# Two-layer block in fp32r: operand halves sent through TensorE together, with the opening, the SSD/GLA order and the last gain rearranged

## The chip, the cores and the metric

The kernel runs on one core of one Trainium2 chip. The metric is device time in microseconds (us) of the whole program. Every matmul of a projection is done in the type float32r: a float32 operand is split into a high part (the value as float32r rounds it) and a low part (what is left), and three products (high by high, high by low, low by high) are accumulated in PSUM.

## What is computed

The program is two transformer-like blocks over 256 tokens (272 with 16 meta tokens in the first block) of width 1024, and a final norm. What the change touches is in these lines of the reference:

```python
# first block
h = xn @ w_in                                    # k, v, q, c, h, b, gates
out = merged @ w_out
u, g = jnp.split(xn @ w_up_gate, 2, axis=-1)     # 2 x 2816 columns
ffn = (jax.nn.gelu(causal_dwconv(u, w)) * g) @ w_down
# second block, layer one: SSD scan and gated linear attention (GLA)
u = h @ w_in                                     # z, x, B, C, dt, q, k, v, gates
out = jnp.concatenate([y_a, o_b], axis=-1) @ w_out
x = x + out
# second block, layer two: attention with a gate, then the final norm
x = x + (attention * gate) @ w_out
```

## The kernel before

**Operands.** Activations lie transposed in SBUF: 128 channels on the partitions, tokens along the free axis. `xhi`/`xlo` hold the high and low part of the normalised input of a stage (8 pieces `kt` of 128 channels), `yhi`/`ylo` those of the branch outputs; `fhi`/`flo` (22 pieces, FFN) and `ehi`/`elo` (16 pieces, second block) are views of the same buffers.

**Weights.** All weights come as one stream of 253 chunks of 128 x 1024 float32 (8 blocks of 128 x 128), in the order of `STREAM` (line 124). SyncE (SP) loads a chunk into one of 4 raw buffers. ScalarE (ACT) makes the high part (`split_hi`, L559), VectorE (DVE) the low part (`split_lo`, L1063), each into a ring of 4 (`RING`). `feed(tile)` on either engine splits as many chunks as the tile has, always the next in the stream, about four tiles ahead. A raw buffer is free when the low part is made, a ring slot when TensorE (PE) has read the chunk.

**Tiles.** A tile is 128 output channels. `project` (L1724) runs over its blocks and issues three matmuls a block, each with a 128 x 128 weight block as the stationary operand and 256 to 272 tokens as the moving one (L1749). For `ev` and `mv` the tokens are stationary and 256 or 512 weight columns move (L1752). `project_together` (L1759, L1777) takes three tiles at once where the input is still being made. Outputs rotate through PSUM banks 0 to 3; `bank_free` lets PE wait until the tile that used the bank before was read (`taken`). Tile names: `k v q c h b gc ga pc pa wo` (mixer), `fu fg fd` (up, gate, down projection of the FFN), `es eb ec ex eq ek ev ez eg eo1 eo2` (SSD and GLA layer, eo1 and eo2 being the two halves of its output projection), `mk mv mq mz mo` (last layer).

**Order.** Each engine has its own program written out by hand; semaphores join them. The places that matter:

- Opening: SP loads half of chunk 0, x in three pieces, the other half, chunk 1. ACT waits for the parameters (L591), makes the high parts (L600, L597), DVE the low parts (L1092, L1078). PE runs tile `k0`, then `k1`, `k2`, then the sum of squares `total(1, 0)` (L1788), then `k3`.
- FFN loop on DVE (L1338 to L1345), for tile pair `i`: `ffn_up` (L1313), `feed(fg i-1)`, `ffn_conv` (two operations, L1320), `ffn_out(i-1)` (L1328), `feed(fu i)`. GpSimd (POOL) scales the gelu (L443) and makes the low part of the result (L449).
- `out_tiles` (L1251): DVE copies each tile of `wo` and `fd` out of PSUM (L1259).
- SSD/GLA loop, `p` = 0 to 3 (DVE L1509, ACT L918, PE L2053): per `p` two SSD head pairs (`turn_x`, `ssd_heads`) and one GLA pair (`turn_keys`, `gla_scores`, `gla_kv`, `gla_out`, `gla_sums`) between the projections. POOL forms the arguments of the GLA exponentials (`gla_args`, L506, L508) and the products with queries and keys (L494, L496).
- Output projection of that layer on DVE: for `eo1` a multiply out of PSUM (L1594), a feed, an addition to H (L1602); for `eo2` `residual` (L1576): addition to H out of PSUM (L1580), feed, low part of the next input (`x_low_of`, L1078). ACT makes the high part and the square, POOL adds the squares (L435). The next tile `mk0` needs all eight pieces of that input.
- The tail: DVE adds `mo` to H (L1699), ACT squares and multiplies with the final gain (L1030, L1039), two sums (L2176, L2179), scaling (L1710), stores.

`d.settle()` makes DVE wait for its own last signalled operation.

Of the kernel before, what the change touches and what calls it, by code (L numbers as in the profile page):

```python
# [138 lines left out]
for _name, _n in (("g_pre_mix", 8), ("g_post_mix", 8), ("g_pre_ffn", 8), ("g_post_ffn", 8), ("even_norm", 8),  # L139
# [19 lines left out]
def build(nc, xT, params, weights, masks, gate_w2, out, scratch):  # L159
    with ExitStack() as ctx:  # L160
# [13 lines left out]
        xhi_t = sb("x_hi", KT * T, F32R)  # L174
        xlo_t = sb("x_lo", KT * T, F32R)
        YW = 3 * KT * NA
        yhi_t = sb("y_hi", YW, F32R)
        ylo_t = sb("y_lo", YW, F32R)
        h_t = sb("hidden", KT * T)
# [5 lines left out]
        rcol = sb("rinv_by_token", 4)  # L185
        arena = sb("arena", ARENA)
# [8 lines left out]
        xhi, xlo, H = v3(xhi_t[:], KT), v3(xlo_t[:], KT), v3(h_t[:], KT)  # L195

        yhi = yhi_t[:].rearrange("p (s a b) -> p s a b", s=3, a=KT)
        ylo = ylo_t[:].rearrange("p (s a b) -> p s a b", s=3, a=KT)
        fhi, flo = v3(yhi_t[:, 0:FT * L], FT), v3(ylo_t[:, 0:FT * L], FT)
        ehi, elo = v3(yhi_t[:, 0:16 * L], 16), v3(ylo_t[:, 0:16 * L], 16)  # L200
# [56 lines left out]
        fy = A4(2, L)  # L257

# [127 lines left out]
        HALF = {t: n for n, t in enumerate((s_, i_) for s_, i_, b_, n_ in STREAM if s_ in ("eb", "ec", "ex", "ez", "eg"))}  # L386
        CONVS = [t for t in HALF if t[0] in ("eb", "ec", "ex")]
        K_TAKEN = [taken[FIRST_OUT["ek", p]][1] for p in range(4)]
# [5 lines left out]
        def _(sp_):  # L394
            half = CW // 2
            cuts = (0, 2 * T, 4 * T, KT * T)

            def load_x(n):
                sp_.dma_start(h_t[:, cuts[n]:cuts[n + 1]], xT[:, cuts[n]:cuts[n + 1]]).then_inc(S(f"load_x{n}"), 16)

            sp_.dma_start(raw[:, 0:half], weights[0, :, 0:half]).then_inc(S("load_half"), 16)
            load_x(0)
            load_x(1)
            sp_.dma_start(raw[:, half:CW], weights[0, :, half:CW]).then_inc(S("raw0"), 16)
            load_x(2)
            for c in range(1, NCHUNKS):
# [17 lines left out]
        def _(pool):  # L424
# [87 lines left out]
            for p in range(4):  # L512
                if p:
                    ssd_weights(2 * p)
                else:
                    gla_args(0)
# [8 lines left out]
                if p:  # L525
                    ssd_add(2 * p)
# [1741 lines left out]
```

## Time and profile before

| | us |
|---|---|
| median of 3 runs | 850.49 (849.14 to 850.52) |
| the profiled execution, own time | 848.99 |
| its span | 847.2 |
| PE busy | 830.6 |
| DVE busy | 620.8 |
| ACT busy | 499.1 |
| POOL busy | 132.7 |

The span is what the trace shows from the first to the last instruction; 1.8 us of the execution lie outside it. A matmul's duration in the trace is its passage through the array and overlaps the next one; what it costs is the distance from its start to the start of the next. So cadences are read from starts, not from durations.

### The profile page before, as it was taken

How to read it: one execution, taken by the hardware profiler on the slowest of the kernel's cores; microseconds unless marked ns; L12 is line 12 of the kernel's file. 1: busy time of each engine (PE TensorE's matmuls, PEld its weight loads, DVE VectorE, ACT ScalarE, POOL GpSimd, SP SyncE). 2: the span in 40 equal slices, each digit the busy share in tenths (PEclk: the TensorE clock that was granted, in tenths of full speed). 3: DMA queues.
4: the chain of work that ended last, by engine and by line, in shares of the span. 5: the costliest groups of instructions: out<-in, count | busy, mean ns of one | idle time of the engine just before them, and what ended most of it. 6: DMA issues, size and time to landing. Idle time of an engine off the chain costs nothing.

```text
span 847.2 us, 16833 instructions
## 1 busy us (share of the span) xinstructions
PE 830.6 (98%) x6770; PEld 800.5 (94%) x6770; DVE 620.8 (73%) x1044; ACT 499.1 (59%) x842; POOL 132.7 (16%) x131
## 2 busy tenths in 40 slices
PE   8999999999999999999999999889999999999997
PEld 7999999999999999999999999779999999888896
DVE  6547888886666688667664488997887697568764
ACT  7346657555454576555554469668768555346655
POOL 1000000000000305433441100332534011000002
PEclk9999999999999999999999999999999999999999
DMA  8754434346555536656566535455454375554431
GB/s 326 233 153 139 152 106 173 127 137 179 183 188 186 173 106 191 201 177 186 189 197 196 180 100 171 142 170 167 150 167 157 112 231 183 186 169 141 126 101 50
DMA packets 39565, 139.81 MB, mean 165 GB/s; under 512 B 4400, under 2 KB 5056, under 8 KB 39360
## 3 DMA queue, kind: packets, MB, share of 16 engines
q1 hardware_dynamic: 37728, 135.78, 50.1%
q10 hardware_dynamic: 1760, 2.96, 1.1%
q8 instruction: 54, 0.88, 0.4%
q14 instruction: 23, 0.19, 0.1%
HBM read 137.65 MB, written 1.06 MB: 164 GB/s over the span
## 4 chain that ended last, share of the span: by engine, by line
PE 90%; DVE 5%; ACT 2%; DMA 1%; issue 1%; SPq 0%; DVEq 0%; ACTq 0%
PE ps L1749 71%; PE ps L1777 5%; PE ps L1752 5%; DVE weights_lo L1063 1%; PE ps L1870 1%; PE ps L1855 1%; PE ps L1884 1%; PE ps L2127 1%; PE ps L2145 1%; PE ps L1998 1%; DMA hidden<-xT_in 1%; PE ps L2135 1%; DVE arena L1375 1%; PE ps L2041 0%; PE ps L2050 0%
## 5 line engine op out<-in xcount | busy, mean ns | idle before, releaser
L1749 PE MATMUL ps<-x_hi,weights_hi 128*128 128x256 f32 (+3 forms) x1288 | 373.0, 290 | 5.4 <-DVE weights_lo L1063 3.0
L1063 DVE TENSOR_TENSOR weights_lo<-raw_weights,weights_hi 128x1024 fp32r<-128x1024 f32 x251 | 311.5, 1245 | 85.4 <-ACT weights_hi L559 85.3
L1749 PE MATMUL ps<-x_lo,weights_hi 128*128 128x256 f32 (+3 forms) x1288 | 363.8, 282 | 0.0
L1749 PE MATMUL ps<-x_hi,weights_lo 128*128 128x256 f32 (+3 forms) x1288 | 363.2, 282 | 0.0
L559 ACT ACTIVATE weights_hi<-raw_weights 128x1024 fp32r<-128x1024 f32 x251 | 263.8, 1053 | 152.8 <-PE ps L1749 62.2
L1749 PEld LDWEIGHTS ps<-x_hi,weights_hi 128*128 128x128 f32 x1288 | 242.9, 189 | 13.6 <-issue 10.9
L1749 PEld LDWEIGHTS ps<-x_lo,weights_hi 128*128 128x128 f32 x1288 | 242.9, 189 | 1.0 <-issue 0.7
L1749 PEld LDWEIGHTS ps<-x_hi,weights_lo 128*128 128x128 f32 x1288 | 243.4, 189 | 0.0
L1749 PE MATMUL ps<-y_hi,weights_hi 128*128 128x256 f32 (+1 forms) x488 | 137.7, 282 | 0.0
L1749 PE MATMUL ps<-y_lo,weights_hi 128*128 128x256 f32 (+1 forms) x488 | 137.4, 282 | 0.0
L1749 PE MATMUL ps<-y_hi,weights_lo 128*128 128x256 f32 (+1 forms) x488 | 137.1, 281 | 0.0
L435 POOL TENSOR_TENSOR arena<-arena 128x256 f32<-128x256 f32 (+1 forms) x24 | 25.9, 1078 | 494.8 <-ACT arena L708 328.2
L1749 PEld LDWEIGHTS ps<-y_hi,weights_hi 128*128 128x128 f32 x488 | 92.0, 189 | 0.3 <-issue 0.2
L1749 PEld LDWEIGHTS ps<-y_lo,weights_hi 128*128 128x128 f32 x488 | 91.9, 188 | 0.3 <-issue 0.2
L1749 PEld LDWEIGHTS ps<-y_hi,weights_lo 128*128 128x128 f32 x488 | 92.0, 189 | 0.0
L443 POOL TENSOR_TENSOR arena<-arena,rinv 128x256 f32<-128x256 f32 x22 | 32.9, 1496 | 81.6 <-ACT arena L751 81.4
L1752 PE MATMUL ps<-weights_hi,x_hi 128*128 128x256 f32 (+1 forms) x96 | 31.0, 323 | 0.0
L1752 PE MATMUL ps<-weights_lo,x_hi 128*128 128x256 f32 (+1 forms) x96 | 30.6, 319 | 0.0
L1752 PE MATMUL ps<-weights_hi,x_lo 128*128 128x256 f32 (+1 forms) x96 | 30.6, 318 | 0.0
L746 ACT ACTIVATE arena<-arena,params 128x256 f32<-128x256 f32 x22 | 11.1, 510 | 30.2 <-DVE arena L1313 30.2
L1313 DVE TENSOR_TENSOR arena<-ps,rinv 128x258 f32<-128x258 f32 x22 | 9.4, 428 | 25.1 <-PE ps L1749 24.5
L1320 DVE SCALAR_TENSOR_TENSOR arena<-arena,params 128x256 f32<-128x256 f32 x44 | 21.9, 498 | 4.2 <-ACT arena L746 1.0
(265 smaller groups left out, 1049.6 us busy)
## 6 DMA issues: line engine op xcount, KB each, us to landing
raw_weights<-weights_in SPq DMA_DIRECT2D x252, 512.0 KB, 3.7
arena<-decay_rows ACTq DMA_DIRECT2D x8, 256.0 KB, 3.6
masks<-masks_in SPq DMA_DIRECT2D x1, 1186.0 KB, 8.3
hidden<-xT_in SPq DMA_DIRECT2D x2, 272.0 KB, 4.1
hidden<-xT_in SPq DMA_DIRECT2D x1, 544.0 KB, 5.6
raw_weights<-weights_in SPq DMA_DIRECT2D x2, 256.0 KB, 4.0
gate_w<-gate_w_in ACTq DMA_DIRECT2D x1, 256.0 KB, 5.7
out<-arena ACTq DMA_DIRECT2D x1, 256.0 KB, 2.1
```

The lines of the kernel that those rows point to most:

```text
L435: ins = nc.gpsimd.tensor_tensor(sq[:, 0, t0:T], sq[:, 0, t0:T], sq[:, i, t0:T], ALU.add)
L443: g.sig(nc.gpsimd.tensor_tensor(fgl[:, i % 2, :], fgl[:, i % 2, :], rinv[:, META:T], ALU.mult), "gelu_scaled")
L559: a.sig(A(whi[:, s * CW:(s + 1) * CW], raw[:, (c % RAW) * CW:(c % RAW + 1) * CW], ACT.Copy), "hi_ready")
L746: a.sig(A(fcv[:, i % 2, :], fu[:, i % 2, 0:L], ACT.Copy, scale=pcol("conv_ffn", i)), "tap_ready")
L1063: d.sig(TT(wlo[:, s * CW:(s + 1) * CW], raw[:, (c % RAW) * CW:(c % RAW + 1) * CW], whi[:, s * CW:(s + 1) * CW].bitcast(F32), ALU.subtract) ...
L1313: d.sig(TT(fu[:, i % 2, :], r, rinv[:, TA:T], ALU.mult), "u_ready")
L1320: ins = STT(out=c_, in0=u[:, j:L + j], scalar=pcol("conv_ffn", FT * j + i), in1=c_, op0=ALU.mult, op1=ALU.add)
L1375: ins = STT(out=dst, in0=scr2[:, n % 2, j:L + j], scalar=pcol("even_conv", 10 * j + ct), in1=dst, op0=ALU.mult, op1=ALU.add)
L1749: ins = mm(bank(BANK_OF[no])[:, 0:b - a], wt, x_[:, kt, a:b], start=s0, stop=s1)
L1752: ins = mm(bank(BANK_OF[no + o])[0:t1 - t0, 0:step * P], x_[:, kt, t0:t1], wt, start=s0, stop=s1)
L1777: ins = mm(bank(BANK_OF[no])[:, 0:b - a], w_[:, at:at + P], x_[:, kt, a:b], start=kt == 0 and n == 0 and len(passes) == 2, stop=kt == KT - ...
L1855: ins = mm(bank(4 + e)[:, c0:c0 + T - t0], keysT[rows, p, k0:k0 + P], qpair[rows, p % 2, t0:T], start=n == 0, stop=n == 2, skip_group_chec ...
```

## The change

1. **Wide tiles.** `x_hi`/`x_lo` and `y_hi`/`y_lo` become the two halves of one buffer each. For the tiles in `WIDE` (fg 2 to 21, fd 0 to 6, eo1 3 to 6, eo2 0 to 6, mo 3 to 6) `project` issues two matmuls a block in place of three: the high weights against high and low tokens as one moving operand of 512 columns into a whole bank, then the low weights against the high tokens, 256 columns, added to the bank's first half. DVE joins the two halves of the bank when it reads the tile: one or two operations more a tile.
2. **Opening.** x comes in four pieces, the first two on ACT's DMA queue with the gain of the first norm in front of them; chunks 0 and 1 come in halves. PE takes `k0` and `k1` together, two pieces of x at a time (`first_keys`), and the sum of squares inside `k3`.
3. **FFN start.** `feed(fu1)` and `feed(fg1)` move one step forward on ACT and DVE.
4. **SSD/GLA loop, p = 0 and 1.** POOL's `gla_args` are gone; DVE makes small columns of biases (`decay_cols`) and ACT forms the exponentials in four pieces of 64 columns each. The products of p = 0 move from POOL to DVE (`first_products`). Gate work of p = 0 moves into p = 1 (`gate_both`). On PE `gla_scores(0)` follows `eq1`, `gla_kv(0)` follows `ek1`, `gla_out(0)` follows `ev1`, and `gla_sums(0)` follows `ez2`.
5. **Tail.** The last piece's multiplication with the final gain moves from ACT to DVE.

```diff
+        WIDE = ([("fd", i) for i in range(KT - 1)] + [("eo1", i) for i in range(3, KT - 1)]
+                + [("eo2", i) for i in range(KT - 1)] + [("mo", i) for i in range(3, KT - 1)]
+                + [("fg", i) for i in range(2, FT)])
...
+                        if tile in WIDE:
+                            b_ = bank(BANK_OF[no])
+                            mm(b_.rearrange("p (c t) -> p c t", c=2), whi[:, at:at + P], x_[:, :, kt, a:b], start=first,
+                               stop=last, skip_group_check=True)
+                            ins = mm(b_[:, 0:L], wlo[:, at:at + P], hi[:, kt, a:b], start=False, stop=last,
+                                     skip_group_check=True)
...
+            def low_part(tile):
+                return bank(BANK_OF[FIRST_OUT[tile]])[:, L:2 * L]
...
                     r = result((stage, i), 0, T - t0)
...
-                    d.sig(V.tensor_copy(mout[:, i, t0:T], r), "mout_ready")
+                    if (stage, i) in WIDE:
+                        d.step(V.tensor_copy(mout[:, i, t0:T], r))
+                        d.settle()
+                        d.sig(TT(mout[:, i, t0:T], mout[:, i, t0:T], low_part((stage, i)), ALU.add), "mout_ready")
+                    else:
+                        d.sig(V.tensor_copy(mout[:, i, t0:T], r), "mout_ready")
...
                 need(dve, "ffn_split", i - 1)
+                if ("fg", i) in WIDE:
+                    d.settle()
+                    d.step(V.tensor_copy(fsum, low_part(("fg", i))))
+                    d.settle()
+                    d.step(TT(fsum, r, fsum, ALU.add))
+                    d.settle()
+                    r = fsum
                 d.sig(TT(fy[:, i % 2, :], r, fgl[:, i % 2, :], ALU.mult), "ffn_y")
...
                     r = result((stage, i), 0, L)
                     d.settle()
+                    if (stage, i) in WIDE:
+                        d.step(TT(H[:, i, META:T], r, H[:, i, META:T], ALU.add))
+                        r = low_part((stage, i))
+                        d.settle()
                     d.sig(TT(H[:, i, META:T], r, H[:, i, META:T], ALU.add), "h_ready")
...
-                d.sig(TT(t_, r, rpost[:, 0:L], ALU.mult), "eo1_taken")
+                if ("eo1", i) in WIDE:
+                    d.step(V.tensor_copy(t_, r))
+                    d.settle()
+                    d.sig(TT(t_, t_, low_part(("eo1", i)), ALU.add), "eo1_taken")
+                    d.settle()
+                    d.step(TT(t_, t_, rpost[:, 0:L], ALU.mult))
+                else:
+                    d.sig(TT(t_, r, rpost[:, 0:L], ALU.mult), "eo1_taken")
...
+            def first_keys():
+
+                for n in range(4):
+                    for c in range(2):
+                        no = FIRST_OUT["k", c]
+                        if n == 0:
+                            pe.wait_ge(S("lo_half"), c + 1)
+                        if n == 2:
+                            pe.wait_ge(S("lo_ready"), c + 1)
+                        for kt in (2 * n, 2 * n + 1):
+                            pe.wait_ge(S("x_split"), kt + 1)
...
+            first_keys()
+            project(("k", 2), x2, 0, T)
+            project(("k", 3), x2, 0, T, first_total)
...
+            def first_products():
+                dve.wait_ge(S("gla_exp"), 1)
+                d.sig(TT(kb[:, 0, :], kb[:, 0, :], e_k[:, 0, :], ALU.mult), "gla_kl")
+                d.sig(TT(ka[:, 0, :], ka[:, 0, :], e_k[:, 0, :], ALU.mult), "gla_ka")
+                for e in range(2):
+                    rows = slice(64 * e, 64 * e + 64)
+                    d.step(TT(qg[rows, 0, e, :], eg[rows, 0, :], e_q[rows, 0, :], ALU.mult))
+                    ins = TT(qe[rows, 0, e, :], em[rows], e_q[rows, 0, :], ALU.mult)
+                    d.sig(ins, "gla_qk") if e else d.step(ins)
...
-                a.step(A(em, ka[:, k, :], ACT.Exp, scale=-1.0 / 16))
-                a.step(A(kb[:, k, :], kb[:, k, :], ACT.Exp, scale=-1.0 / 16))
-                a.settle()
-                a.step(A(ka[:, k, :], ka[:, k, :], ACT.Exp, scale=1.0 / 16))
+                for n, (dst, scale) in enumerate(((kb[:, k, :], 1.0 / 16), (ka[:, k, :], 1.0 / 16), (em, -1.0 / 16))):
+                    for c in range(4):
+                        w_ = slice(64 * c, 64 * c + 64)
+                        a.step(A(dst[:, w_], gcs[:, p, w_], ACT.Exp, scale=scale, bias=decay_cols[:, n, p, c:c + 1]))
...
+                if p == 1:
+                    project(("eq", 1), x2, META, T)
+                    gla_scores(0)
+                    project(("ek", 1), x2, META, T)
+                    turn_x(2)
+                    gla_kv(0)
+                    project(("ev", 1), x2, META, T, toks=toksL)
+                    ssd_heads(2)
+                    gla_out(0)
...
-                a.sig(A(fin[:, c, KT - 1, :], H[:, KT - 1, w_], ACT.Copy, scale=pcol("final_norm", KT - 1)), "gained")
...
+            d.step(TS(fin[:, :, KT - 1, :], H[:, KT - 1, META:T].rearrange("p (c t) -> p c t", c=2),
+                      pcol("final_norm", KT - 1), None, ALU.mult))
```

## Rows read from the trace of the kernel before

**Rows 1.** The page: busy time by engine, and the chain that ended last, by engine.

```profile
PE 830.6 (98%) x6770; PEld 800.5 (94%) x6770; DVE 620.8 (73%) x1044; ACT 499.1 (59%) x842; POOL 132.7 (16%) x131
PE 90%; DVE 5%; ACT 2%; DMA 1%; issue 1%; SPq 0%; DVEq 0%; ACTq 0%
```

**Rows 2.** Waits of PE: line, releaser, us in total, times, longest.

```profile
PE ps L1749 <- DVE weights_lo L1063: 3.0, 2, 2.4
PE ps L2041 <- DVE arena L1472: 2.4, 1, 2.4
```

**Rows 3.** Timeline of PE: start us, duration us, instruction; tile fd4 and mv.

```profile
460.98 0.27 PE L1749 MATMUL ps<-y_hi,weights_hi 128*128 128x256 f32 x1
...
468.75 0.28 PE L1749 MATMUL ps<-y_hi,weights_hi 128*128 128x256 f32 x1
...
730.23 0.40 PE L1752 MATMUL ps<-weights_hi,x_hi 128*128 128x512 f32 x1
...
750.14 0.39 PE L1752 MATMUL ps<-weights_lo,x_hi 128*128 128x512 f32 x1
```

**Rows 4.** Windows: length, busy us of PE, PEld, DVE, ACT, POOL, PE clock, DMA.

```profile
520.00:540.00 20.00, 19.48 (x160) 18.47 (x158) 18.44 (x32) 16.42 (x32) 1.13 (x2) 1.00 0.62 194
540.00:560.00 20.00, 16.59 (x124) 14.91 (x124) 18.97 (x28) 11.58 (x24) 8.56 (x9) 0.91 0.42 139
680.00:700.00 20.00, 20.00 (x172) 20.00 (x171) 18.93 (x27) 11.24 (x18) 3.21 (x4) 1.00 0.72 234
```

**Rows 5.** Timeline of the opening: DVE low parts, first matmul of k4.

```profile
5.30 0.69 DVE L1092 TENSOR_TENSOR weights_lo<-raw_weights,weights_hi 128x512 fp32r<-128x512 f32 x1 [5.30 <-ACT weights_hi L600]
5.91 1.73 DVE L1078 SCALAR_TENSOR_TENSOR x_lo<-hidden,params,x_hi 128x272 fp32r<-128x272 f32 x4
...
21.34 0.29 PE L1749 MATMUL ps<-x_hi,weights_hi 128*128 128x272 f32 x1
```

**Rows 6.** Timeline of the SSD/GLA loop, p = 0 and 1: PE, ACT, DVE.

```profile
542.08 0.36 PE L1749 MATMUL ps<-x_hi,weights_hi 128*128 128x256 f32 x1 [2.41 <-DVE weights_lo L1063]
...
540.41 0.42 ACT L892 ACTIVATE arena<-arena 128x256 f32<-128x256 f32 x1 [2.18 <-POOL arena L508]
...
537.47 1.27 DVE L1400 TENSOR_TENSOR_SCAN arena<-masks,arena 128x256 f32<-128x256 f32 x2
...
540.72 1.21 DVE L1063 TENSOR_TENSOR weights_lo<-raw_weights,weights_hi 128x1024 fp32r<-128x1024 f32 x1
...
573.81 0.36 PE L1749 MATMUL ps<-x_hi,weights_hi 128*128 128x256 f32 x1
```

**Rows 7.** Timeline of one FFN round on DVE, and a POOL scaling.

```profile
387.34 0.43 DVE L1313 TENSOR_TENSOR arena<-ps,rinv 128x258 f32<-128x258 f32 x1 [1.56 <-PE ps L1749]
...
390.26 1.22 DVE L1063 TENSOR_TENSOR weights_lo<-raw_weights,weights_hi 128x1024 fp32r<-128x1024 f32 x1
393.04 0.43 DVE L1313 TENSOR_TENSOR arena<-ps,rinv 128x258 f32<-128x258 f32 x1 [1.56 <-PE ps L1749]
...
390.54 1.53 POOL L443 TENSOR_TENSOR arena<-arena,rinv 128x256 f32<-128x256 f32 x1 [3.29 <-ACT arena L751]
```

**Rows 8.** Groups of DVE instructions by form: count, busy us, mean ns.

```profile
L1259 DVE COPY arena<-ps 128x256 f32<-128x256 f32 x8 | 3.4, 425 | 11.1 <-PE ps L1749 10.1 <-ACT arena L714 1.0
```

**Rows 9.** Timeline of eo1, eo2 and mk: DVE, then the first matmul of mk1.

```profile
678.65 0.43 DVE L1602 TENSOR_TENSOR hidden<-hidden,arena 128x256 f32<-128x256 f32 x1
679.18 0.42 DVE L1594 TENSOR_TENSOR arena<-ps,rinv_post 128x256 f32<-128x256 f32 x1
...
692.27 0.42 DVE L1580 TENSOR_TENSOR hidden<-ps,hidden 128x256 f32<-128x256 f32 x1
...
694.81 0.42 DVE L1580 TENSOR_TENSOR hidden<-ps,hidden 128x256 f32<-128x256 f32 x1
...
706.10 0.48 DVE L1078 SCALAR_TENSOR_TENSOR x_lo<-hidden,params,x_hi 128x256 fp32r<-128x256 f32 x1 [0.58 <-ACT x_hi L567]
...
707.85 0.47 PE L1749 MATMUL ps<-x_hi,weights_hi 128*128 128x256 f32 x1
```

More of the change, by code:

```diff
@@ L760, in _ @@
             ffn_gelu(0)
+            feed(("fg", 1))
             ffn_gelu(1)
[L762 removed]
             ffn_high(0)
@@ new lines, in gate_both @@
+            def gate_both(u):
+                z_full(("ez", u), zs[:, u % 2, :])
+                z_full(("eg", u), gs[:, u % 4, :])
+                gate_y(u)
+            dve.wait_ge(S("tkc_ready"), 1)
+            ssd_args(0)
+            ssd_weights(0)
+            split_lo()
+            z_full(("ex", 1), xs[:, 1, :], name="xsilu")
+            z_half(("ez", 0), zs[:, 0, :])
+            feed(("ez", 0))
+            ssd_y(0)
+            gate_sum()
+            decay_sums(0)
+            feed(("eg", 0))
@@ new lines, in _ @@
+            z_half(("eg", 0), gs[:, 0, :])
+            ssd_weights(1)
+            ssd_args(1)
+            conv_in(("ex", 2))
+            feed(("ex", 2))
+            first_products()
+            z_half(("ez", 1), zs[:, 1, :])
+            feed(("ez", 1))
+            conv_rest(("ex", 2), 2, xs[:, 2, :])
+            ssd_y(1)
+            z_half(("eg", 1), gs[:, 1, :])
+            gla_scores(0)
+            z_full(("ex", 2), xs[:, 2, :], name="xsilu")
+            feed(("eg", 1))
+            conv_in(("ex", 3))
@@ new lines, in _ @@
+            ssd_args(2)
+            gla_states(0)
+            feed(("ex", 3))
+            for p in range(1, 4):
+                u = 2 * p
+                take_queries(p)
+                if p == 1:
+                    take_keys(1)
+                    gate_both(0)
+                    feed(("eq", 1))
+                    conv_rest(("ex", 3), 3, xs[:, 3, :])
+                    ssd_y(2)
+                    feed(("ek", 1))
+                    z_full(("ex", 3), xs[:, 3, :], name="xsilu")
+                    gate_both(1)
+                    feed(("ev", 1))
+                    z_half(("ez", 2), zs[:, 0, :])
+                    ssd_args(3)
+                    gla_norm(0)
+                    feed(("ez", 2))
+                    ssd_low(0)
+                    ssd_low(1)
+                else:
@@ L2097, in last_scan @@
                     gla_out(3)
-            project_together([("eo1", i) for i in range(3)], ehi, elo, [(0, L)] * 3,
+            project_together([("eo1", i) for i in range(3)], e2, [(0, L)] * 3,
                              lambda kt: pe.wait_ge(S("ye_hi"), kt + 1),
@@ L2167, in _ @@
             together = 3
-            project_together([("mo", i) for i in range(together)], ehi, elo, [(0, L)] * together,
+            project_together([("mo", i) for i in range(together)], e2, [(0, L)] * together,
                              lambda kt: pe.wait_ge(S("mo_hi"), kt + 1),
```

443 lines of the change are left out of this document (228 added, 215 removed).

## The prediction

> **What bounds the kernel now.** I read the page first: PE is busy for 98% of the span and makes up 90% of the chain that ended last [rows 1]. So a microsecond counts only where PE issues fewer or cheaper passes, or waits less. The waits of PE come next: the two largest sums, 3.0 and 2.4 us, are single waits of 2.4 us each plus crumbs, and both end with DVE, once with the low part of a weight chunk, once with the GLA states [rows 2]. The windows by stage say where: between 520 and 560 us DVE is busy 18.4 and 19.0 of 20 us, and PE loses time there and nowhere else by more than a microsecond or two; the second of these windows also has a granted clock of 0.91, which is some 3.5 us at 1.2 GHz in place of 2.4 GHz, after PE had stood idle. A third window is the one to keep in mind: at 680 to 700 us PE is busy all the time, and DVE 18.93 of 20 us [rows 4]. DVE is nearly a second bound there, unseen by the chain.
>
> Last, the cadence of PE, since a duration in the trace overlaps the next pass. Tile fd4 has 66 passes of 256 columns from 460.98 to 468.75: 117.7 ns each. In mv, 86 passes of 512 columns run from 730.23 to 750.14: 231.5 ns each [rows 3]. Two narrow passes cost 235.4 ns, one of double width 231.5.
>
> The measurement can tell about 0.2%, 1.7 us, from no change.
>
> **Wide tiles, on PE.** Each block turns three passes (353 ns) into one of 512 and one of 256 columns (349 ns), so 3.9 ns are saved. Blocks: fg 20 x 8 = 160, fd 7 x 22 = 154, eo1 4 x 8 = 32, eo2 7 x 8 = 56, mo 4 x 8 = 32, together 434. That is 434 x 3.9 ns = 1.7 us, and the columns fed are as many as before. By the same rows the bounds are 0 and, if the whole 11 ns by which a narrow pass exceeds 256 columns at 2.4 GHz (106.7 ns) went with the third weight load, 4.8 us. I take 1.7, because mv shows this very width.
>
> Page sentences, which the sum does not use. The trace gives 117.7 and 231.5 ns [rows 3]. The Trainium skill, "TensorE: Matmul & The Clock Gate", section "Back-to-back issue gap", gives N/2.4 + 2.5 ns for an isolated stream; an estimate by that page is 2.5 ns saved a block, 1.1 us in all.
>
> **Wide tiles, on DVE: fg.** In the FFN a round of DVE starts with L1313 at 387.34 and ends with the feed of 390.26, over at 391.48; with 0.1 us for the settle it could begin again at 391.58, but waits for PE until 393.04 (1.56 us idle before) [rows 7]. So a round takes 4.24 us of PE's 5.70 us. New in it are a copy out of PSUM (0.425 us, [rows 8]) and an addition; a dependent operation of this size costs 0.53 us from start to start (678.65 to 679.18, [rows 9]), and one more settle goes in front of the copy: 2 x 0.53 + 0.18 = 1.24, so 5.48 us. Against POOL: its scaling takes 1.53 us where it meets DVE's feed (390.54, feed over at 391.48, so 0.6 us of its own) [rows 7]; today that ends in DVE's idle time, later it will not. I lay it on the new round and find the multiply put off by about 0.1 and the next feed by 0.15 us. DVE's round is then about 5.73 us against PE's 5.70 - 0.03 = 5.67. PE's gain in these 20 tiles (0.6 us) is lost and about 0.6 us more. The earlier `feed(fu1)` and `feed(fg1)` take out some 0.5 to 0.8 us of today's starts of the loop. FFN up and gate: 0 in sum, from -1 to +5 (a round of 5.95).
>
> **fd and mo.** A tile of fd lasts 7.8 us on PE and has idle DVE beside it; mo's last tile stays narrow. -0.6 and -0.15 us. If the last mo additions were late, +0.5.
>
> **eo1 and eo2, the place that decides.** DVE comes out of the GLA work of the last pair late and catches up through these tiles: it works without a pause until 705.5, and the last x_low comes at 706.10 behind ACT's x_hi (0.58 us idle); PE, with that, starts mk1 at 707.85 with no stall to speak of [rows 9]. The change adds on this chain 2 x 0.53 us for each of 4 tiles of eo1 and 0.53 us for each of 7 of eo2: 4.24 + 3.71 = 7.95 us. One eo2 round is 2.54 us today (692.27 to 694.81) and becomes 3.07, above PE's 24 passes = 2.83 us: the backlog no longer shrinks, it grows. What is queued behind: the feeds, so that eo1_7 to eo2_2 each start 0.3 to 0.9 us later (2.0 in sum), and at the end the eighth x_low, at 706.1 + 7.95 - a few tenths of ACT's wait it would have had anyway = about 714.5. `mk0` needs it. So mk1 starts 7.7 us later; less 0.35 us of wide passes: +7.35 us (6 to 8.5). In mk0 PE would stand for about 6 us with a few passes between. After the 2.41 us of idle before 542.08 the clock fell for 3.5 us [rows 4, 6]; here I expect the same, +1.4 us (0 to 1.8).
>
> **SSD/GLA order.** Today eg1 starts at 542.08 on a chunk whose low part DVE began at 540.72 [rows 6], because `gate_sum` (as long as a split), both scans (1.27 us from 537.47, [rows 6]) and `ssd_weights(1)` sit in front of that feed. These move behind it, so DVE can begin the split at about 536.2, where `gate_sum` stands today, and the chunk is there at 537.4, before PE needs it. The GLA exponentials wait 2.2 us for POOL (540.41, [rows 6]); with biases instead they wait only for the scans, and `gla_out(0)`, whose wait is the other 2.4 us, gets ev1 and two heads in front of it (6.5 us of PE work as cover). ACT's price is 12 short pieces for 3 long ones, about 1 us a pair, which lies beside other work. DVE takes on four POOL products (1.7 us) and hands two `gate_y` groups to p = 1. Laying PE, DVE, ACT and POOL out step by step with the durations of today's operations, PE has waits of about 0.5 us (bank of ex3, on `z_half(eg0)`) and 0.3 us (ev1), and reaches eg2 at 566.8 in place of 573.81 [rows 6]. Of these 7.0 us 5 are the two waits, 1.7 the clock that no longer falls, the rest small waits. I take -6.5 for what a later round may take back (-3 to -8.3).
>
> **Opening.** DVE starts at 5.30 and needs 0.69 us for a half chunk and 0.43 for a piece of x [rows 5]: 4 x 0.69 + 8 x 0.43 = 6.2, to 11.5; nine passes of 0.127 us are left for k0 and k1: 12.7. k2 runs to 15.8; k3 waits for its low part (squares come first) to about 16.1; k4, today at 21.34 [rows 5], would start at 20.2, held by the bank of k0. -1.1 us (-0.5 to -1.9). **Tail**: ACT's second scaling comes 0.3 us earlier but DVE is not waiting for it: 0 (-0.2 to 0.3).
>
> **Sum**, against the profiled execution (848.99 us, 847.2 of span and 1.8 around it): -1.1 + 0 - 0.6 - 6.5 + 7.35 + 1.4 - 0.15 = +0.4, so 849.4 us. The median of three stands 1.5 us above that execution, which gives 850.9 us.
>
> **Rivals.**
> A, the backlog costs nothing: DVE makes up in eo1 and eo2 what is added, by a shorter joint operation or because its work comes earlier. For it: PE shows no stall there today. Against: DVE is busy 18.93 of 20 us [rows 4]. Then 850.9 - 7.35 - 1.4 = 842.1; partly true it ends between.
> B, the weight load is what a narrow pass pays for. The sum would have 11 ns a block: only fd and mo (186 blocks) could use it, the others stand behind DVE; 186 x 7 ns = 1.3 us more, 849.6. Against: passes of 512 columns have 18 ns over 213.3, more, not less. The Trainium skill, same page and section, goes further and gives 131 ns a pass at N=512 in a sustained stream; by that an estimate would be 40 us faster, and the 231.5 ns here speak against it.
> C, slower: POOL and DVE collide more than I laid out, and the FFN round of DVE is 5.95 us. It decides from 5.67 us on. 20 x 0.28 = 5.6 us in place of 1.2: 855.3. For it: a POOL operation that meets one of DVE's takes 0.6 us of its own behind it [rows 7], and that can happen twice a round. Against: only operations with both inputs in SBUF met it so, and the two new ones read PSUM. [...]
> D, slower: the SSD/GLA order brings half, because another wait (keys turned, then scores, then states) takes the place of the one removed: 854.2.
>
> **How the numbers follow.** Forecast 0.48 (spread 848 to 853.5: faster 0.14, same 0.25, slower 0.09), A 0.17, B 0.10 (0.03 faster, 0.07 same), C 0.13, D 0.12. Faster 0.34, same 0.32, slower 0.34. The forecast's own range is 847 to 854; taken out to most of A and C it is 843 to 856, which leaves 2 in 10 outside. Both signs hold much, since two terms of about 7 us cancel.
>
> **What would show it.** Right: the wide passes start 231 ns apart and the narrow ones behind them 118; the FFN round grows from 5.70 to about 5.73 and its DVE idle on PE vanishes; DVE is busy without a pause from 677 to the last x_low, mk0 waits for x_low for several us and the clock falls behind it; between 520 and 560 no wait of PE above 1 us and a clock of 1.0. Wrong: no wait in mk0 (A), wide passes far below 231 ns (B), FFN rounds near 6 us (C), a new wait of PE on states or scores near 550 (D).

## The result and the profile after

The changed kernel takes **855.47 us** (median of 4 runs, 854.94 to 855.98) against 849.82 us: ratio 1.0067, 95% interval 1.0053 to 1.0081, so 5.65 us slower. The forecast was 850.9 us, in the range 843 to 856, with a chance of 0.34 for slower. The time lies inside the range, at its upper end. The likeliest case was not what happened, and the middle of the forecast was off by 4.6 us; that the range held is owed to its width, which was drawn to take in rival C at 855.3 us.

The profiled execution took 854.94 us, of which 853.1 are span, against 848.99 and 847.2. From the page of the changed kernel, its busy times and the chain that ended last by engine, to be held against [rows 1]:

```profile
PE 832.2 (98%) x6336; PEld 781.2 (92%) x6336; DVE 652.5 (76%) x1121; ACT 506.0 (59%) x876; POOL 111.9 (13%) x119
PE 78%; DVE 13%; ACT 5%; issue 2%; POOL 1%; DMA 1%; DVEq 0%; SPq 0%; ACTq 0%; POOLq 0%
```

434 passes are gone from PE (6770 to 6336), yet it is busy for longer. DVE is busy for 32 us more, and its share of the chain went from 5% to 13%. PE's waits, to be held against [rows 2] (line, releaser, total us, times, longest):

```profile
PE ps L1853 <- DVE x_split L1104: 4.2, 3, 2.4
PE ps L2146 <- ACT arena L879: 1.5, 1, 1.5
PE ps L1844 <- DVE arena L1365: 1.3, 2, 1.0
PE ps L2168 <- DVE arena L1513: 1.3, 1, 1.3
...
PE ps L2116 <- DVE arena L1488: 0.9, 2, 0.5
```

Both waits of 2.4 us of [rows 2] are gone. Five kinds stand in their place: x_low for mk0 (L1853), the turned keys for the scores (L2146), a bank that the joined gate tile frees (L1844), the GLA states (L2168) and y before the turn of x (L2116). The windows, to be held against [rows 4]:

```profile
540.00:560.00 20.00, 18.82 (x161) 17.49 (x161) 18.83 (x37) 15.61 (x43) 2.84 (x2) 1.00 0.46 152
...
580.00:600.00 20.00, 17.59 (x150) 16.97 (x151) 18.16 (x36) 12.80 (x31) 2.04 (x2) 1.00 0.45 145
...
700.00:720.00 20.00, 15.76 (x105) 14.65 (x104) 14.22 (x20) 9.03 (x16) 2.37 (x3) 0.83 0.51 158
```

PE is better off at 540 to 560 us (busy 18.82 for 16.59, clock 1.00 for 0.91), worse at 580 to 600 (busy 17.59; it was full before), and loses 4.2 us at 700 to 720 us with a clock of 0.83.

**Where the time went.** The last pass of every projection tile, taken from both traces and subtracted (after minus before), gives a ledger; for eg2 it is the first pass. A table of it, in us:

| stretch | forecast | measured |
|---|---|---|
| opening, to k4 | -1.1 | -0.85 |
| FFN up and gate | 0 | +0.67 |
| fd | -0.6 | -1.0 |
| SSD/GLA, to the start of eg2 | -6.5 | -6.74 |
| SSD/GLA, from there to the end of eo1_0 | (in the same -6.5) | +5.47 |
| eo1, eo2 and mk to mk1, stall and clock together | +8.75 | +8.57 |
| mo | -0.15 | -0.24 |
| sum | +0.4 | +5.9 |

One line of seven is wrong by more than a microsecond: most of what the SSD/GLA order gained, the same stage gave back. The opening's gain is the least certain line: in the traces of experiments 1 to 12, which all have the same new opening, k4 ends only 0.2 to 0.8 us earlier than in the kernel before.

### The profile page after: what moved, and what is told of

It reads as the page before. It is cut to its first block, busy times and chain, and to the rows that moved or that the text cites. A ratio compares the mean times of both kernels' runs of the same rounds, so it can differ in the third digit from the quotient of the medians.

```text
span 853.1 us, 16082 instructions
## 1 busy us (share of the span) xinstructions
PE 832.2 (98%) x6336; PEld 781.2 (92%) x6336; DVE 652.5 (76%) x1121; ACT 506.0 (59%) x876; POOL 111.9 (13%) x119
## 4 chain that ended last, share of the span: by engine, by line
PE 78%; DVE 13%; ACT 5%; issue 2%; POOL 1%; DMA 1%; DVEq 0%; SPq 0%; ACTq 0%; POOLq 0%
PE ps L1853 47%; PE ps L1844 9%; PE ps L1882 5%; DVE weights_lo L1086 5%; PE ps L1846 5%; PE ps L1856 3%; ACT weights_hi L558 1%; PE ps L1997 1%; PE ps L1982 1%; PE ps L2011 1%; PE ps L2265 1%; PE ps L2283 1%; DVE arena L1412 1%; DVE x_split L1104 1%; PE ps L2273 1%
## 5 line engine op out<-in xcount | busy, mean ns | idle before, releaser
L1853 PE MATMUL ps<-x_split,weights_hi 128*128 128x256 f32 (+3 forms) x2224 | 413.9, 287 | 5.4 <-DVE x_split L1104 4.2
L1853 PEld LDWEIGHTS ps<-x_split,weights_hi 128*128 128x128 f32 x2224 | 343.0, 189 | 15.2 <-issue 6.6
L1853 PE MATMUL ps<-x_split,weights_lo 128*128 128x256 f32 (+3 forms) x1112 | 313.6, 282 | 0.0
L1853 PEld LDWEIGHTS ps<-x_split,weights_lo 128*128 128x128 f32 x1112 | 210.3, 189 | 0.0
L1844 PE MATMUL ps<-y_split,weights_hi 128*128 128x512 f32 x274 | 96.2, 394 | 0.1
L1853 PE MATMUL ps<-y_split,weights_hi 128*128 128x258 f32 (+1 forms) x428 | 77.3, 282 | 0.7 <-DVE weights_lo L1086 0.7
L1846 PE MATMUL ps<-y_split,weights_lo 128*128 128x256 f32 x274 | 76.7, 280 | 0.0
L1853 PEld LDWEIGHTS ps<-y_split,weights_hi 128*128 128x128 f32 x428 | 66.0, 189 | 1.1 <-issue 1.0
L1844 PEld LDWEIGHTS ps<-y_split,weights_hi 128*128 128x128 f32 x274 | 51.3, 187 | 12.1 <-issue 0.9
L1853 PE MATMUL ps<-y_split,weights_lo 128*128 128x258 f32 (+1 forms) x214 | 60.3, 282 | 0.0
L1844 PE MATMUL ps<-x_split,weights_hi 128*128 128x512 f32 x160 | 56.9, 394 | 1.3 <-DVE arena L1365 1.3
L1846 PEld LDWEIGHTS ps<-y_split,weights_lo 128*128 128x128 f32 x274 | 51.8, 189 | 0.3 <-issue 0.2
L1853 PEld LDWEIGHTS ps<-y_split,weights_lo 128*128 128x128 f32 x214 | 40.4, 189 | 0.0
L1844 PEld LDWEIGHTS ps<-x_split,weights_hi 128*128 128x128 f32 x160 | 30.0, 188 | 7.7 <-DVE arena L1365 1.8
L1846 PEld LDWEIGHTS ps<-x_split,weights_lo 128*128 128x128 f32 x160 | 30.1, 188 | 0.0
```

What stands on the lines that cost most here:

```text
L1844: mm(b_.rearrange("p (c t) -> p c t", c=2), whi[:, at:at + P], x_[:, :, kt, a:b], start=first, stop=last, skip_group_check=True)
L1846: ins = mm(b_[:, 0:L], wlo[:, at:at + P], hi[:, kt, a:b], start=False, stop=last, skip_group_check=True)
L1853: ins = mm(bank(BANK_OF[no])[:, 0:b - a], wt, v_[:, kt, a:b], start=s0, stop=s1)
```

## Experiments

The question is twofold: do the joins of eo1 and eo2 cost what the ledger says, and what took back the gain of the order? Each change below is against the changed kernel, unless said otherwise. The ratios are to the kernel before, which was timed again beside experiments 1 to 4 (850.22 us), 5 to 8 (850.37), 9 and 10 (849.27) and 11 and 12 (850.53). So between experiments of different groups a difference below about a microsecond says nothing.

**1. No wide tile.**

```
-        WIDE = ([("fd", i) for i in range(KT - 1)] + [("eo1", i) for i in range(3, KT - 1)]
...
+        WIDE = []
```

> The changed kernel with no wide tile at all; the opening, the order of the SSD/GLA stage and the last norm stay as changed. Theory of the joins: the two traces put +8.75 us between the end of eo1_0 and the end of mk_1 on the joins of eo1 and eo2 with the clock that falls behind the stall, +0.68 us on gate tiles 2 to 5, -1.0 on fd and -0.2 on mo. All of it goes away, what stays is -0.86 (opening) and -1.3 (SSD/GLA): 2.2 us under the kernel before, about 847.6 us, granted clock 1.00 after the first mk tile. Rival, the order: the stall ahead of mk_0 comes from the changed order of the feeds and the split of weights, not from the joins; then it stays and the time is 853 to 856 us.

Measured: 846.87 us (ratio to the kernel before 0.9965, 0.9952 to 0.9978). The stall of mk0 is gone and the clock after it is 1.00, so the changed feeds are not what makes it. All wide tiles together cost 8.6 us; what is left of the change is a gain of about 3 us.

**2. Wide everywhere but in eo1 and eo2.**

```
-        WIDE = ([("fd", i) for i in range(KT - 1)] + [("eo1", i) for i in range(3, KT - 1)]
-                + [("eo2", i) for i in range(KT - 1)] + [("mo", i) for i in range(3, KT - 1)]
-                + [("fg", i) for i in range(2, FT)])
+        WIDE = ([("fd", i) for i in range(KT - 1)] + [("mo", i) for i in range(3, KT - 1)] + [("fg", i) for i in range(2, FT)])
```

> The changed kernel with fg, fd and mo wide, eo1 and eo2 as before. Theory of the joins: the 8.75 us behind eo1_0 go, the rest of the ledger stays: -0.86 (opening) +0.68 (fg) -1.0 (fd) -1.3 (SSD/GLA) -0.2 (mo) = -2.7 us, about 847.1 us. Rival, the order: the stall before mk_0 stays and the time is about 855 us. Rival, the gate joins cost more than the trace shows (VectorE is later for all that follows): over 848.5 us.

Measured: 846.69 us (0.996, 0.9945 to 0.9974). The loss stands or falls with the wide tiles of eo1 and eo2. The other 31 tiles bring next to nothing in this form, since the gate tiles lose at their start what they win later (experiment 11).

**3. Wide in eo1 and eo2 alone.**

```
+        WIDE = ([("eo1", i) for i in range(3, KT - 1)] + [("eo2", i) for i in range(KT - 1)])
```

> The changed kernel with only eo1_3 to eo1_6 and eo2_0 to eo2_6 wide. Theory of the joins: -0.86 (opening) -1.3 (SSD/GLA) +8.75 (eo and mk_0) = +6.6 us, about 856.4 us, with a TensorE wait on x_split of about 4 us and a granted clock near 0.83 in one 20 us window behind it. Rival: joins of eo are covered when VectorE isn't made late by the gate tiles: under 852 us.

Measured: 856.16 us (1.0072, 1.0057 to 1.0087); the wait for x_low is 4.2 us in 3 as in the changed kernel. So the 11 tiles cost 9.3 us over experiment 1, whatever the gate tiles do.

**4. The SSD/GLA stage in its old order**: feeds, exponentials, GpSimd products, turns and scores on all engines as in the kernel before. All other parts as changed.

```
-                if p == 1:
-                    project(("eq", 1), x2, META, T)
-                    gla_scores(0)
...
+                if p:
                     project(("eq", p), x2, META, T)
                     turn_x(u)
                     gla_kv(p - 1)
```

> The changed kernel with the SSD/GLA stage in the order of the kernel before (feeds, GLA products on GpSimd, key turns and scores where they were), everything else as changed. By the trace of the changed kernel the order is worth 1.3 us net by the end of that stage: 855.5 + 1.3 = about 856.8 us. By the recorded sum it is worth 6.5 us: about 862 us. Rival: the backlog of VectorE is carried over into the eo tiles, so that nothing of the order's gain or loss is left at the end: 855.5 us.

Measured: 856.86 us (1.0077, 1.0061 to 1.0094). The order is worth 1.4 us, near the 1.3 of the ledger, not 6.5. The window at 540 to 560 us is back at PE 16.64 of 20 us busy and a clock of 0.91. The profiled execution took 858.62 us, the other three 856.45 to 857.00. In its trace the clock is 0.91 from 560 to 580 us as well, behind the wait of 2.4 us for the GLA states; behind the same wait the trace of the kernel before has 1.00.

**5. Filler ahead of mk0.** PE works on constants while it waits.

```
-            project(("mk", 0), x2, META, T, x_ready(3 * KT))
+            def filled(kt):
+                if kt < 3:
+                    stay_busy((3, 5, 3)[kt])
+                x_ready(3 * KT)(kt)
+
+            project(("mk", 0), x2, META, T, filled)
```

> The changed kernel, all tiles wide, with 3, 5 and 3 matmuls of constants on TensorE ahead of row blocks 0, 1 and 2 of mk_0, in the gaps where it waits for x_split (4.2 us in 3 waits); their results are not used. Theory of the clock: the stall itself stays, since VectorE sets it, but TensorE is not idle before mk_0 and the granted clock stays at 1.00 instead of 0.53 and 0.61 in the 4 us windows behind 708 us; the half-speed passes of mk_0 and mk_1 (about 1.7 us) come back: 853.8 us, and the wait of 4.2 us reads as busy filler. Rival, the clock is no cost of its own: 855.5 us or, with a filler that runs on when the data is there, up to 857 us.

Measured: 853.2 us (1.0039, 1.0024 to 1.0053), 2.3 us less than the changed kernel with the same late x_low. Windows of 4 us, first the changed kernel, then this one:

```profile
704.00:708.00 4.00, 1.59 (x12) 1.18 (x10) 3.86 (x6) 2.53 (x5) 0.79 (x1) 1.00 0.61 216
708.00:712.00 4.00, 2.17 (x7) 1.86 (x8) 2.55 (x5) 1.82 (x4) 0.79 (x1) 0.53 0.48 155
712.00:716.00 4.00, 4.00 (x20) 3.66 (x19) 1.71 (x3) 1.84 (x3) 0.00 (x0) 0.61 0.46 131
```

```profile
704.00:708.00 4.00, 4.00 (x23) 3.61 (x22) 3.86 (x6) 2.33 (x5) 0.80 (x1) 1.00 0.65 206
708.00:712.00 4.00, 3.53 (x25) 3.17 (x25) 2.55 (x5) 2.02 (x4) 0.80 (x1) 1.00 0.52 172
712.00:716.00 4.00, 4.00 (x34) 3.95 (x33) 2.93 (x4) 2.40 (x4) 0.00 (x0) 1.00 0.37 121
```

DVE's column is the same in the first two windows of both. PE's clock stays at 1.00 and it issues 34 passes instead of 20 between 712 and 716 us. So of the loss at mk0 2.3 us are the clock by the medians (1.8 between the two profiled executions, 854.94 and 853.16), and the rest is the late x_low.

**6. Wide in eo1 alone**, 4 tiles.

```
+        WIDE = [("eo1", i) for i in range(3, KT - 1)]
```

> Only eo1_3 to eo1_6 wide (4 tiles, their join two more VectorE instructions each, +4.24 us of VectorE time by the recorded sum); eo2 (7 tiles, +3.71 us) as before. Theory: VectorE is the only engine behind mk_0, so its added time comes through one for one, +4.2 us over the kernel without wide tiles (846.9), and about 1 to 1.5 us of clock behind the stall: 851.5 to 852.5 us. Rival, slack: VectorE still has idle time in the eo2 tiles that swallows the first tiles' joins: under 850 us. Rival, all or nothing: the stall is made by the first late tile, 855 us.

Measured: 850.21 us (1.0001, 0.9992 to 1.001), 3.3 us over experiment 1, less than I expected. PE waits 1.5 us in 2 for x_low, and the clock stays at 1.00 (windows from 704 us on), so no clock is paid. That leaves 3.3 us for 4 joins, each of three instructions in place of one.

**7. Keys and states first.** In the kernel of experiment 1, for p = 1, ScalarE takes the turned keys before the high part of y and the tap, and VectorE makes the GLA states before the decay sums.

```
                     feed(("ex", u + 2))
+                if p == 1:
+                    take_keys(1)
                 ssd_high(u)
...
                 if p == 1:
+                    gla_states(1)
                     decay_sums(1)
```

> The kernel without wide tiles (846.9 us), and for the head pair p=1 two moves: ScalarE takes the turned keys ahead of the high part of y and the convolution tap, and VectorE makes the GLA states ahead of the decay sums. Theory of order within the stage: the TensorE waits for these two (1.5 us for the keys, 1.3 us for the states) are a matter of what stands ahead in the queue; both go and the time falls by 2.5 to 2.8 us, to 844.3 us. Rival, VectorE as the bound (18.9 and 19.3 of 20 us busy in the windows before): the waits move to the next result of VectorE and less than 1 us is gained: 846 to 847 us.

Measured: 847.73 us (0.9971, 0.9961 to 0.9981), no faster than experiment 1. Its waits of PE in the stage, and its window behind 600 us:

```profile
PE ps L2116 <- DVE arena L1486: 2.0, 1, 2.0
PE ps L2168 <- DVE arena L1511: 1.0, 1, 1.0
PE ps L1856 <- DVE arena L1402: 0.6, 1, 0.6
...
```

```profile
600.00:620.00 20.00, 17.99 (x133) 16.90 (x134) 16.10 (x24) 17.21 (x32) 9.63 (x10) 0.91 0.54 167
```

The wait for the keys is gone and that for the states is 1.0 for 1.3 us; ex5 ends 2.3 us earlier. But the wait for y_4 before the turn of x grew from 0.5 to 2.0 us, and the clock fell behind it. The moved work met a fixed point: y_4 starts at 605.24 us, only 0.6 us earlier than in experiment 1 (605.87). The trace shows which point. DVE, then ACT (start, duration, line; in brackets idle time before and its releaser):

```profile
598.45 1.22 DVE L1084 TENSOR_TENSOR weights_lo<-raw_weights,weights_hi 128x1024 fp32r<-128x1024 f32 x1
601.91 3.40 DVE L1084 TENSOR_TENSOR weights_lo<-raw_weights,weights_hi 128x1024 fp32r<-128x1024 f32 x2 [2.24 <-ACT weights_hi L556]
605.24 0.47 DVE L1486 SCALAR_TENSOR_TENSOR arena<-arena,params,ps 128x256 f32<-128x256 f32 x1
...
597.66 2.96 ACT L895 ACTIVATE arena<-arena,decay_columns 128x64 f32<-128x64 f32 x12
600.52 0.40 ACT L896 ACTIVATE arena<-arena 128x256 f32<-128x256 f32 x1
600.83 1.99 ACT L556 ACTIVATE weights_hi<-raw_weights 128x1024 fp32r<-128x1024 f32 x2
```

The 12 exponentials (2.96 us) keep ACT from the high parts of ev's two weight chunks. DVE stands idle for 2.24 us, makes their low parts, and only then comes y_4 (L1486). The same idle time of 2.24 us stands in the trace of experiment 1.

**8. Less work on VectorE.** In the kernel of experiment 1, eight low parts are 128 columns wide.

```
+        LESS = {FIRST_BLOCK[t] // BPC for t in (("ez", 0), ("eg", 0), ("ex", 2), ("ez", 1), ("eg", 1), ("ex", 3), ("eq", 1),
+                                                ("ek", 1))}
...
-                s = c % RING
+                s, w_ = c % RING, P if c in LESS else CW
```

> The kernel without wide tiles (846.9 us), and the low part of eight weight chunks (ez_0, eg_0, ex_2, ez_1, eg_1, ex_3, eq_1, ek_1) is only made for 128 of 1024 columns: part of the computation is left out, some 8 us of VectorE between 535 and 575 us. Theory, VectorE as the bound of the first half of the stage: all five TensorE waits of the stage between 540 and 600 us (0.6 + 0.6 + 1.5 + 1.3 and the 0.3 to 0.9 ahead of them) go: 842.5 to 843.5 us. Rival, the waits are a matter of order on ScalarE and of the chain of exponentials: the 1.5 us for the keys and most of the rest stay, 845.5 to 846.9 us.

Measured: 845.18 us (0.9945, 0.993 to 0.996), 1.7 us less than experiment 1, between the two forecasts and nearer to the rival. PE is busy for all of 540 to 560 us, and in the stretch from 540 to 620 us its two large waits are untouched:

```profile
PE ps L2146 <- ACT arena L879: 1.5, 1, 1.5
PE ps L2168 <- DVE arena L1513: 1.4, 1, 1.4
PE ps L2116 <- DVE arena L1488: 0.5, 1, 0.5
```

Some 8 us of relief (an estimate: 8 low parts of 1.22 us, of which an eighth is left) for a DVE that is busy 19 of 20 us bought 1.7 us. The amount of DVE's work between 535 and 575 us is at most a small part of what took the gain back; that a busy engine is the bound was the wrong reading.

**9. The weights of ev first.** In the kernel of experiment 7, ACT makes both high parts before the exponentials, for p = 2 and 3.

```
+                    feed(("ev", p))
                     gla_exps(p)
-                    feed(("ev", p))
```

> The kernel before this one (no wide tiles, keys taken and GLA states made earlier for p=1; 847.7 us), and for p=2 and 3 ScalarE makes the high parts of the two weight chunks of ev ahead of the exponentials of the decays, 12 instructions and 2.96 us in one piece, instead of behind them. In its trace VectorE stands idle for 2.24 us for these high parts, its low parts (3.40 us) follow, and y_4 behind them; TensorE waits 2.0 us for that, and the clock is 0.91 in the 20 us behind 600 us. Theory, that chain took the gain of the two moves: the 2.0 us wait and the lower clock go, the 2.3 us gained at ex_5 stay, and the same wait for p=3 (0.5 us) goes: 847.7 - 2.0 - 1 - 0.5 = 844.2 us, at least under 845.5. Rival, VectorE or the GLA products on GpSimd behind the later exponentials are the next to be late: a wait moves on to the keys of p=2 and the time stays over 846.5 us.

Measured: 849.75 us (1.0003, 0.9993 to 1.0012), 2.0 us slower than experiment 7. The wait for y_4 is gone. The wait for the states has grown from 1.0 us, and two others are new:

```profile
PE ps L2168 <- DVE arena L1511: 2.3, 2, 1.3
PE ps L2137 <- DVE arena L1519: 2.0, 2, 1.0
PE ps L2125 <- POOL arena L486: 1.6, 2, 1.4
```

The states (L2168), the turn of the keys (L2137), whose bank the GLA norm has to read first, and the SSD heads (L2125), for which GpSimd makes the weights, all hang on what ACT does behind the exponentials, which now end 2.7 us later. My theory named the right instructions and the wrong remedy: with both orders something on ACT is late.

**10. Experiment 9 with a short list of wide tiles.**

```
+        WIDE = ([("fd", i) for i in range(KT - 1)] + [("mo", i) for i in range(3, KT - 1)]
+                + [("fg", i) for i in range(6, FT)])
```

> The same, with fd_0 to fd_6, mo_3 to mo_6 and the gate tiles from fg_6 on wide, and eo1 and eo2 not. By the rates of the traces (0.145 us per fd tile, 0.05 per mo tile, 0.04 per gate tile, and no wait at fg_5 since that tile is not wide): -1.0 -0.2 -0.6 = 1.8 us under the kernel without wide tiles of the same order, 842.4 us if that gives 844.2. Rival, the saving of a wide pass is a shift within the trace and the joins take it back: no difference.

Measured: 848.15 us (0.9982, 0.9973 to 0.9992), 1.6 us under experiment 9. The absolute forecast missed, for it stood on experiment 9; the difference is near the 1.8 us that the saving by tile in the traces had given.

**11. The short list of experiment 10 in the order of the change**, without the moves of experiments 7 and 9.

> The changed kernel in its own SSD/GLA order, with only fd_0 to fd_6, mo_3 to mo_6 and the gate tiles from fg_6 on wide: no wide tile in eo1 and eo2, none where the gate tiles start up. In the order of the run before it, the same set of tiles took 1.6 us off (849.75 to 848.15). Theory, the saving of wide passes adds to the rest: 846.9 - 1.6 = 845.3 us, below both kernels. Rival, with fg_2 to fg_5 wide as well the gain was only 0.2 us (846.87 to 846.69), and this is the measure of all wide passes outside eo: 846.5 us or more.

Measured: **845.34 us** (0.9941, 0.9926 to 0.9956). This is below both kernels: 1.5 us under experiment 1, some 5 us under the kernel before. It differs from experiment 2 only in fg_2 to fg_5, and is 1.35 us below it. PE's largest wait between 320 and 345 us, first in experiment 2 (gate tiles wide from fg_2), then in this one (from fg_6):

```profile
PE ps L1842 <- DVE arena L1363: 1.4, 2, 1.0
...
```

```profile
PE ps L1852 <- DVE arena L1364: 0.4, 1, 0.4
...
```

The joins of fg_2 to fg_5 fall where DVE has not caught up yet with the start of the FFN: PE waits 1.0 us less for the banks that they free.

**12. Three exponentials for twelve.** In the kernel of experiment 7, for p = 2 and 3; the chunks of 64 columns share one bias there, so part of the scaling is left out.

```
-                    for c in range(4):
-                        w_ = slice(64 * c, 64 * c + 64)
+                    for c in range(4 if p < 2 else 1):
+                        w_ = slice(64 * c, 64 * c + 64) if p < 2 else slice(0, L)
```

> The kernel with the keys taken and the states made earlier for p=1 (847.7 us), and for p=2 and 3 each of the three exponentials of the decays is one instruction of 256 columns with one bias instead of four of 64 columns with four: the scaling by chunk is left out there. ScalarE is 2.96 us in 12 instructions; three of 256 columns take some 0.4 us each, 1.7 us less, twice. Theory, the chain ScalarE exponentials - high parts of ev's weights - low parts - y_4 set the 2.0 us wait: it falls to 0.3 us or less, the lower clock behind it goes, for p=3 the 0.5 us wait goes: 844 to 845 us. Rival, what is queued on VectorE itself is late as well and another wait comes up: over 846.5 us.

Measured: 844.48 us (0.9929, 0.9913 to 0.9946), 3.25 us less than experiment 7 with the same work but for 2 x 1.66 us on ACT. (The nine executions of experiment 7 spread from 846.68 to 847.92 us, so the gain is 2.2 to 3.4 us.) Its exponentials, and all its waits of PE from 540 to 672 us:

```profile
597.82 1.30 ACT L895 ACTIVATE arena<-arena,decay_columns 128x256 f32<-128x256 f32 x3
```

```profile
PE ps L2168 <- DVE arena L1511: 1.0, 1, 1.0
PE ps L1856 <- DVE arena L1402: 0.6, 1, 0.6
PE ps L1856 <- issue: 0.3, 1, 0.3
PE ps L1853 <- DVE arena L1474: 0.2, 1, 0.2
```

The wait of 2.0 us is gone with the lower clock behind it (1.00 in the window at 600 to 620 us), and none came in its place. That shows that the exponentials, as 12 short instructions, turned the gain of the keys and the states into a wait.

## Why the prediction was right and wrong

**Right: the place that decides.** "eo1 and eo2" were forecast at +7.35 and the clock at +1.4, together 8.75 us; the ledger has +8.6, and experiment 3 against experiment 1 gives 9.3. The steps on the way hold too, with sizes off in both directions. (The recorded 714.5 us for the last x_low is not what its sum gives: 706.1 + 7.95 less a few tenths is about 713.8. The 7.7 us and the term of 7.35 us do not hang on it.) A joined eo1 round lasts 3.04 us where an ordinary one lasts 2.12, from the starts of the additions:

```profile
680.07 0.42 DVE L1694 TENSOR_TENSOR hidden<-hidden,arena 128x256 f32<-128x256 f32 x1
680.60 0.42 DVE L1680 COPY arena<-ps 128x256 f32<-128x256 f32 x1
681.06 0.42 DVE L1682 TENSOR_TENSOR arena<-arena,ps 128x256 f32<-128x256 f32 x1
681.52 0.43 DVE L1684 TENSOR_TENSOR arena<-arena,rinv_post 128x256 f32<-128x256 f32 x1
...
683.11 0.43 DVE L1694 TENSOR_TENSOR hidden<-hidden,arena 128x256 f32<-128x256 f32 x1
...
686.15 0.42 DVE L1694 TENSOR_TENSOR hidden<-hidden,arena 128x256 f32<-128x256 f32 x1
...
688.27 0.42 DVE L1694 TENSOR_TENSOR hidden<-hidden,arena 128x256 f32<-128x256 f32 x1
```

That is 0.92 us for a join of two instructions, 0.46 each, not the 0.53 that I took from start to start in [rows 9]. The 0.53 us stand behind an addition with both inputs in SBUF (680.07 to 680.60 here, 678.65 to 679.18 there); the added operations read PSUM, and the next one starts 0.46 us after them (680.60, 681.06, 681.52). So 4 x 0.92 + 7 x 0.46 = 6.9 us and not 7.95. DVE works through without a pause until it waits for ACT, as foreseen:

```profile
710.31 0.49 DVE L1104 SCALAR_TENSOR_TENSOR x_split<-hidden,params,x_split 128x256 fp32r<-128x256 f32 x1 [0.58 <-ACT x_split L566]
```

The clock cost more than the 1.4 us taken over from the other stall: 1.8 to 2.3 by experiment 5. The two misses nearly cancel, which is luck: 8.57 for 8.75 us is closer than the terms deserve. Rival A (the backlog is free) is refuted by experiments 1 to 3, down to the 4 tiles of experiment 6.

**Right in kind, small: PE's saving.** The forecast was 3.9 ns a block. From the first pass of fd5 to that of fd6 in the changed kernel are 7.63 us:

```profile
467.86 0.39 PE L1844 MATMUL ps<-y_split,weights_hi 128*128 128x512 f32 x1
...
475.49 0.39 PE L1844 MATMUL ps<-y_split,weights_hi 128*128 128x512 f32 x1
```

Over 22 blocks that is 346.8 ns, against 7.77 / 22 = 353.2 ns in [rows 3]: 6.4 ns a block, and 1.0 us in fd. This sum of 231.5 and 117.7 ns (349.2) is too long by 2.4 ns; the cadence of a pure stream of either width did not carry over to a mix of both. Rival B (11 ns a block) does not come about. By the Trainium skill, "TensorE: Matmul & The Clock Gate", section "Back-to-back issue gap", 131 ns a pass at N=512 would put a block far below 346.8 ns; the trace speaks against it for this data type.

**Wrong by 0.7 us, inside its bounds: FFN.** The steady rounds are better than forecast. DVE's round was laid out at 5.73 us against PE's 5.67; PE stayed the bound with 0.31 us to spare:

```profile
381.78 0.43 DVE L1343 TENSOR_TENSOR arena<-ps,rinv 128x258 f32<-128x258 f32 x1 [0.31 <-PE ps L1853]
...
387.44 0.43 DVE L1343 TENSOR_TENSOR arena<-ps,rinv 128x258 f32<-128x258 f32 x1 [0.31 <-PE ps L1853]
...
384.97 0.74 POOL L461 TENSOR_TENSOR arena<-arena,rinv 128x256 f32<-128x256 f32 x1 [2.91 <-ACT arena L752]
386.52 1.20 POOL L467 TENSOR_TENSOR y_split<-arena,y_split 128x256 fp32r<-128x256 f32 x1 [0.81 <-ACT y_split L756]
```

POOL's scaling, 1.53 us long beside DVE's feed in [rows 7], takes 0.74 us; it now runs beside DVE's copy and addition and not beside the feed. The Trainium skill, "SBUF — State Buffer", section "Who interferes with whom", says that a VectorE instruction with two inputs in SBUF contends with a GpSimd instruction that reads SBUF, and that one with at most one input there does not, outside the two-port modes; the trace agrees with 0.74 us beside operations that read PSUM. The collision has not gone but moved: the feed (385.92 to 387.13 us) now meets POOL's next operation, the low part, which takes 1.20 us where it took 0.73 (392.22 us in the trace of the kernel before). It is off PE's path. So rival C does not come about, and where the forecast had PE's gain lost to the collision, a steady round ends 0.03 us earlier than before. The loss is at the start of the loop: fg_5 ends 1.2 us later for a bank, which the forecast left out, and experiment 11 shows that it goes with the joins of fg_2 to fg_5.

**Wrong: "SSD/GLA order", -6.5 us.** The step as far as it was laid out is right: eg2 starts at 565.88 in place of 573.81, 6.7 us of it from this stage (forecast 7.0). What failed is the sentence "I take -6.5 for what a later round may take back (-3 to -8.3)": half a microsecond was set aside where 5.5 were taken. The layout ended at eg2, and the price of ACT, "about 1 us a pair, which lies beside other work", was wrong in both halves. It is 12 pieces in 2.96 us where three long ones take 1.30 (experiment 12), 1.7 us a pair, in all four pairs and not only in the two that were laid out; and it is in front of the weights of ev. From eg2 on, the ledger has new waits of 1.5 us (keys), 1.3 us (states) and twice 0.5 us (y before the turn), 3.8 of the 5.5 us. Another 1.0 us is lost in the group of SSD matmuls behind ez3, which took 0.88 us in the kernel before (at 582.64 us):

```profile
574.72 1.86 PE L2125 MATMUL ps<-arena 128*64 128x256 f32 x8
```

0.4 us of that is a wait for POOL's SSD weights in the middle of the group. The rest, some 0.7 us, stays unassigned.

This is rival D, "another wait (keys turned, then scores, then states) takes the place", down to the names. It had a chance of 0.12, and 854.2 us for half the order. With all but 1.3 us of the order's gain gone, the time came to 855.5.

**What remains of a chain.** The expectations of experiments 7 and 8 name two explanations, the order on a queue and the sheer load of DVE. Neither was enough alone. Moving both pieces of work forward (7) took the keys' wait away and 0.3 us of the states', and brought nothing; taking 8 us of load away (8) brought 1.7 us; and only both moves together with a shorter ACT step (12) brought 2.4 us over experiment 1. How much of it the exponentials would bring in the order of experiment 1, without the moved keys and states, was not tried.

One reading of the prediction is too wide: that PE loses time between 520 and 560 us "and nowhere else by more than a microsecond or two". In the first 20 us it is busy for 16.44. The opening has its own term, so no sum changes.

## What to carry to other kernels

A change that spares TensorE a few nanoseconds a pass and pays for it with joins on VectorE is to be laid where VectorE has idle time in every round, and not in the rounds in which it catches up: the 314 wide blocks of fd, mo and the gate tiles from fg_6 on gained 1.5 us, the 88 in eo1 and eo2 lost 9. When a reordering removes a wait, lay the queues out to the end of the stage, not to the point where the gain is largest; a gain in the middle of a loop is a forecast for that point only. And a splitting of one long instruction into short ones is to be counted by its length (2.96 for 1.30 us) and by what is queued behind it.

## What the runs showed of the hardware

A wait of PE can cost more than its length. x_low, late by 4.2 us in 3 waits with a few passes between them, had a granted clock of 0.53 and 0.61 behind it from 708 to 716 us, so for most of that time the lower of the two levels, 1.2 GHz. That cost 1.8 to 2.3 us more, and with filler passes in the gaps the clock stayed at 1.00 (experiment 5). A single wait of 2.0 us that ended at 605.85 us also had a window at 0.91 around it (experiment 7), while 1.5 us in 2 waits left the clock at 1.00 (experiment 6), and so did the waits of 1.5 and 1.3 us, 12 us apart, in the changed kernel. The price of one and the same wait is not fixed: behind the 2.4 us for the GLA states the clock was 1.00 in the trace of the kernel before and 0.91 in that of experiment 4.

This is a part of why four joins cost 3.3 us and eleven 9.3. DVE's added work is 3.7 us for the four and 6.9 for the eleven, and only the eleven had a clock to pay.

On VectorE, with 128x256 elements and 0.42 to 0.43 us each, an operation that waits for the one before it starts 0.46 us after it where that one read PSUM, and 0.53 us after it where that one had both inputs in SBUF (680.07 to 681.52 us in the changed kernel, 678.65 to 679.18 in [rows 9]). What makes the difference was not tested.
